# Second block, latent mixer and its memory attention: rotary and memory scores from stacks of high parts and remainders over all 128 rows

## The reference, cut to what matters

```python
def mla_mixer(z, cos, sin, qa_g, kva_g, w_uq, w_ukv, qn_g, kn_g):
    ...
    q = rms_norm_2(q, qn_g)
    k = rms_norm_2(k, kn_g)
    q = jnp.concatenate([q[..., :MLA_NOPE], apply_rope(q[..., MLA_NOPE:], cos, sin)], axis=-1)
    k = jnp.concatenate([k[..., :MLA_NOPE], apply_rope(k[..., MLA_NOPE:], cos, sin)], axis=-1)
    o = causal_block_attention(q, k, v)

def memory_attention(qm, mem_n, w_mem_kv, qn_g, kn_g):
    kv = mem_n @ w_mem_kv
    q = rms_norm_2(qm.reshape(B, S, MEM_HEADS, MEM_HDIM), qn_g)
    k = rms_norm_2(kv[..., :MEM_W].reshape(B, M, MEM_HEADS, MEM_HDIM), kn_g)
    ...
```

## Time and profile before

| | |
|---|---|
| median of three runs | 1678.35 us (1676.62 to 1679.75) |
| profiled execution | 1679.82 us, its span 1678.0 us |
| TensorE | busy 1660.4 us (99%), granted clock 0.998 |
| VectorE, ScalarE, GpSimd | busy 896.8, 781.1, 704.5 us |
| HBM | 150.15 MB read, 91 GB/s over the span |

### The profile page before, as it was taken

How to read it: one execution, slowest core, us unless ns; L and a number is a source line. 1 busy time by engine, 2 the same in 40 slices (tenths; PEclk the granted TensorE clock), 3 DMA queues, 4 the chain that set the end, 5 groups by cost and what they waited for, 6 DMA issues and landing times.

```text
span 1678.0 us, 24465 instructions
## 1 busy us (share of the span) xinstructions
PE 1660.4 (99%) x8381; PEld 1361.3 (81%) x8381; DVE 896.8 (53%) x1718; ACT 781.1 (47%) x1213; POOL 704.5 (42%) x372
## 2 busy tenths in 40 slices
PE   9999999999999999999999999999999999999999
PEld 6788678888987899888888888888767888888887
DVE  6799877558426487646555531152554555555100
ACT  6323566337454545445545432345564455445222
POOL 4344212444634576344444444444202444444445
PEclk9999999999999999999999999999999999999999
DMA  6233211433422210233333333322201323333333
GB/s 223 76 113 107 76 39 62 153 100 104 137 89 88 76 39 26 64 89 100 100 92 96 99 101 101 112 95 88 64 1 51 89 100 100 96 91 100 101 113 113
DMA packets 44381, 153.56 MB, mean 92 GB/s; under 512 B 4976, under 2 KB 5104, under 8 KB 44272
## 3 DMA queue, kind: packets, MB, share of 16 engines
q1 hardware_dynamic: 41184, 145.10, 27.9%
q10 hardware_dynamic: 3120, 7.43, 1.3%
HBM read 150.15 MB, written 2.10 MB: 91 GB/s over the span
## 4 chain that ended last, share of the span: by engine, by line
PE 88%; DVE 4%; issue 4%; POOL 2%; ACT 1%; DMA 0%; POOLq 0%; SPq 0%; ACTq 0%; DVEq 0%
PE DB L1179 9%; PE DB L1178 9%; PE DB L1177 9%; PE DB L744 8%; PE DB L746 8%; PE DB L745 8%; PE DB L1196 5%; PE DB L1198 5%; PE DB L1197 5%; PE SC L873 3%; PE SC L1059 2%; PE DB L893 2%; PE DB L797 2%; POOL WL L644 1%; PE DB L799 1%
## 5 line engine op out<-in xcount | busy, mean ns | idle before, releaser
L644 POOL TENSOR_TENSOR WL<-RAW,WH 128x1024 fp32r<-128x1024 f32 x257 | 618.5, 2407 | 924.8 <-ACT WH L1306 922.1
L1306 ACT ACTIVATE WH<-RAW 128x1024 fp32r<-128x1024 f32 x257 | 272.4, 1060 | 597.5 <-PE DB L746 177.8
L1177 PE MATMUL DB<-XH,WH 128*128 128x512 f32 x640 | 249.0, 389 | 0.0
L1178 PE MATMUL DB<-XL,WH 128*128 128x512 f32 x640 | 249.0, 389 | 0.0
L1179 PE MATMUL DB<-XH,WL 128*128 128x512 f32 x640 | 249.0, 389 | 0.0
L744 PE MATMUL DB<-XH,WH 128*128 128x512 f32 x568 | 228.8, 403 | 3.8 <-POOL WL L644 2.3
L746 PE MATMUL DB<-XH,WL 128*128 128x512 f32 x568 | 221.7, 390 | 0.0
L745 PE MATMUL DB<-XL,WH 128*128 128x512 f32 x568 | 221.4, 390 | 0.0
L1178 PEld LDWEIGHTS DB<-XL,WH 128*128 128x128 f32 x640 | 120.1, 188 | 25.1
L1177 PEld LDWEIGHTS DB<-XH,WH 128*128 128x128 f32 x640 | 120.1, 188 | 24.9
L1179 PEld LDWEIGHTS DB<-XH,WL 128*128 128x128 f32 x640 | 120.1, 188 | 24.9
(11 more groups left out here) (517 smaller groups left out, 2947.9 us busy)
## 6 DMA issues: line engine op xcount, KB each, us to landing
RAW<-in_stream_dram SPq DMA_DIRECT2D x267, 512.0 KB, 3.5
TP<-in_toep_dram ACTq DMA_DIRECT2D x4, 512.0 KB, 3.6
X<-in_xt_dram ACTq DMA_DIRECT2D x1, 2048.0 KB, 13.8
out_dram<-X SPq DMA_DIRECT2D x8, 256.0 KB, 4.3
X<-in_xt_dram ACTq DMA_DIRECT2D x4, 256.0 KB, 6.4
X<-in_xt_dram SPq DMA_DIRECT2D x4, 256.0 KB, 6.1
MRAW<-in_memt_dram ACTq DMA_DIRECT2D x2, 512.0 KB, 4.8
CONST<-in_consts_dram SPq DMA_DIRECT2D x1, 448.0 KB, 8.8
```

What stands on the lines that cost most here:

```text
L644: nc.gpsimd.tensor_tensor(WL[:, s, :], RAW[:, j, :], WH[:, s, :].bitcast(F32), ALU.subtract).then_inc(lo_done, 1)
L1177: mm(o, WH[:, s, c], xh(k), start=(k == 0), stop=False)
L1178: mm(o, WH[:, s, c], xl(k), start=False, stop=False)
L1306: A(WH[:, n % SPLIT, :], RAW[:, n % RING, :], ACT.Copy).then_inc(hi_done, 1)
```

## The change

- The memory queries of layer 1 are stacked: `QMS1` holds for each head its 64 rows rounded, and in the other 64 rows their remainders. The memory keys are held twice, rounded in both halves of the rows (`MKH1`) and as remainders in both halves (`MKL1`). A memory score is now two products of the fast float type over 128 rows, with `MKH1` and with `MKL1`. The two heads no longer wait for one another.
- The rotary queries are stacked in the same way (`QRS`, one tile a head), and the rotary keys, now made over all 128 rows (`KRD` in place of `KR`), are split into `KRH` and `KRL`. A latent score is the float32 product of `QN` and `KN` as before, and two fast products over 128 rows.
- ACT rounds (2 + 4 instructions for the memory, 6 + 6 in `rope_high` for the rotary parts), DVE takes the remainders (4 + 4, and 6 + 6 in `rope_low`). The place of each in its engine's list is seen in the diff. New semaphores join them. The stacks and keys lie where `XH` and `XL` lay, and in free parts of the arena.

```diff
@@ -325,7 +325,6 @@
         QN = at("QN", [P, MLH, TOK], A0 + 0)
         KN = at("KN", [P, MLH, TOK], A0 + 16)
         QR = at("QR", [P, 3, TOK], A0 + 32)
-        KR = at("KR", [P, 3, TOK], A0 + 38)
         MV = at("MV", [P, NT, MLH * P], A0 + 44)
         CQH = at("CQH", [P, 3, TOK], A0 + 44, F32R)
         CQL = at("CQL", [P, 3, TOK], A0 + 50, F32R)
@@ -342,6 +341,13 @@
         POSI = at("POSI", [P, TOK], A0 + 84, I32)
 
         KPR = at("KPR", [P, TOK], A0 + 60)
+        QRS = [at(f"QRS{h}", [P, TOK], A0 + kb, F32R) for h, kb in enumerate((38, 40, 42, 84, 86, 70))]
+        KRD = at("KRD", [P, MLH, TOK], 32)
+        KRH = at("KRH", [P, MLH, TOK], 16, F32R)
+        KRL = at("KRL", [P, MLH, TOK], 32, F32R)
+        QMS1 = at("QMS1", [P, 4, TOK], A0 + 62, F32R)
+        MKH1 = at("MKH1", [P, 4, MEM], 28, F32R)
+        MKL1 = at("MKL1", [P, 4, MEM], 44, F32R)
         YLM = at("YLM", [P, 2, TOK], A0 + 68, F32R)
         HALF = [slice(0, DH), slice(DH, P)]
 
...
@@ -550,7 +564,10 @@
                         r = slice(DH * e, DH * e + DH)
                         h = 2 * p + e
                         c = 8 * p + 2 * i + e
-                        yield dict(rq=RQM[:, c:c + 1], both=RQM[:, c - e:c - e + 2], qk=[(q[r, p, P * i:P * i + P], MKT[l][r, p, :])], w=MEM,
+                        qk = [(q[r, p, P * i:P * i + P], MKT[l][r, p, :])]
+                        if l == 1:
+                            qk = [(QMS1[:, h, P * i:P * i + P], k[:, h, :]) for k in (MKH1, MKL1)]
+                        yield dict(rq=RQM[:, c:c + 1], both=RQM[:, c - e:c - e + 2], qk=qk, w=MEM,
                                    bias=CZ[:, 0:MEM],
                                    v=[MVT[l][:, s, DH * h:DH * h + DH] for s in range(2)],
                                    bank=MOUT[l][p], o=MOUT[l][p][r, P * i:P * i + P], first=(i == 0 and e == 0), last=(i == NT - 1 and e == 1),
@@ -560,12 +577,13 @@
             for j in range(0, MLH, 2):
                 for i in range(NT):
                     for e in range(2):
-                        h, r = j + e, HALF[e]
+                        h = j + e
                         w = P * (i + 1)
                         c = 8 * (h // 2) + 2 * i + h % 2
                         yield dict(rq=HR[:, GROUPS["qn"][0] % 2, c, :],
                                    both=HR[:, GROUPS["qn"][0] % 2, c - e:c - e + 2, 0], qk=[(QN[:, h, P * i:P * i + P], KN[:, h, 0:w]),
-                                       (QR[r, h // 2, P * i:P * i + P], KR[r, h // 2, 0:w])], w=w,
+                                       (QRS[h][:, P * i:P * i + P], KRH[:, h, 0:w]),
+                                       (QRS[h][:, P * i:P * i + P], KRL[:, h, 0:w])], w=w,
                                    bias=CZ[:, TOK - w:TOK],
                                    v=[MV[:, s, P * h:P * h + P] for s in range(i + 1)],
                                    bank=OUT2[e], o=OUT2[e][:, P * i:P * i + P], first=(i == 0), last=(i == NT - 1),
@@ -866,13 +884,17 @@
                         if pair[0]["kind"] == "b" and pair[0]["first"]:
                             pe.wait_ge(kb_low, 1)
                             pe.wait_ge(qs_low, 2 * pair[0]["grp"] + 2)
-                        for a in range(len(pair[0]["qk"])):
-                            for s in pair:
-                                if s["kind"] == "m1" and s is pair[1]:
-                                    pe.wait_ge(qk_done, s["g"])
-                                last = mm(s["score"][:, 0:s["w"]], *s["qk"][a], start=(a == 0), stop=(a == len(s["qk"]) - 1))
-                                if a == len(s["qk"]) - 1:
-                                    last.then_inc(qk_done, 1)
+                        if pair[0]["kind"] == "m1":
+                            pe.wait_ge(mk_low, 4)
+                            pe.wait_ge(qm_low, 4)
+                        if pair[0]["kind"] == "l" and pair[0]["first"]:
+                            pe.wait_ge(kr_low, pair[1]["grp"] + 1)
+                            pe.wait_ge(qr_low, pair[1]["grp"] + 1)
+                        parts = range(len(pair[0]["qk"]))
+                        for a, s in ([(a, s) for s in pair for a in parts] if pair[0]["kind"] == "m1" else itertools.product(parts, pair)):
+                            last = mm(s["score"][:, 0:s["w"]], *s["qk"][a], start=(a == 0), stop=(a == len(s["qk"]) - 1))
+                            if a == len(s["qk"]) - 1:
+                                last.then_inc(qk_done, 1)
                     for _ in range(pieces(k) if beside is not None else 0):
                         next(beside, None)
                     if twos and k >= 4 and k % 2 == 0:
@@ -1762,8 +1784,13 @@
                 head_square(HEADS[f"kn{h}"][1][0], KN[:, h, :])
             evac("qm11", QM1[:, 1, :])
             evacuated("qm11")
+            for e, r in enumerate(HALF):
+                A(QMS1[r, e:4:2, :], QM1[r, :, :], ACT.Copy).then_inc(qm_high, 1)
             for k in range(2):
                 head_square(HEADS[f"qm1{k}"][1][0], QM1[:, k, :])
+            for e, r in enumerate(HALF):
+                for half in (r, HALF[1 - e]):
+                    A(MKH1[half, e:4:2, :], MKT[1][r, :, :], ACT.Copy).then_inc(mk_high, 1)
 
             def key_factors(*heads):
                 for h in heads:
@@ -1777,6 +1804,15 @@
                 b = DB[JOBS[f"uqr{k // 2}"].bank(k % 2)]
                 head_square(HEADS[f"qn{2 * k}"][1][1], b[:, :])
                 A(QR[:, k, :], b[:, :], ACT.Identity, scale=col("qn", 1)).then_inc(act_emptied, 1)
+            def rope_high(k):
+
+                act.wait_ge(roped, 10 + k)
+                for e, r in enumerate(HALF):
+                    A(QRS[2 * k + e][r, :], QR[r, k, :], ACT.Copy).then_inc(qr_high, 1)
+                for h in (2 * k, 2 * k + 1):
+                    act.wait_ge(hs_done, HEADS[f"kn{h}"][0] + 1)
+                    A(KRH[:, h, :], KRD[:, h, :], ACT.Copy).then_inc(kr_high, 1)
+
             kn = HR[:, GROUPS["kn"][0] % 2, 0:24, 0]
             act.wait_ge(kn_sum, 1)
             A(kn, kn, ACT.Sqrt, scale=1.0 / 192).then_inc(kn_std, 1)
@@ -1793,6 +1829,7 @@
                     head_square(HEADS[f"qn{h}"][1][0], QN[:, h, :])
                 if k < 2:
                     key_factors(2 * k + 2, 2 * k + 3)
+                rope_high(k)
             act.wait_ge(kv_std, 1)
             def head_values(k):
                 act.wait_ge(slab_used, JOBS[f"uv{k}"].done)
@@ -2462,20 +2499,42 @@
             V.tensor_tensor(kn.rearrange("p (h t) -> p h t", t=NT), SC[0][:, c:c + 24].rearrange("p (h t) -> p h t", t=NT),
                             KS[:, :, :].broadcast_to([P, MLH, NT]), ALU.add).then_inc(kn_sum, 1)
             query_sums("qm1")
+            for e, r in enumerate(HALF):
+                dve.wait_ge(qm_high, e + 1)
+                for p in range(2):
+                    V.tensor_tensor(QMS1[HALF[1 - e], 2 * p + e, :], QM1[r, p, :], QMS1[r, 2 * p + e, :].bitcast(F32),
+                                    ALU.subtract).then_inc(qm_low, 1)
             dve.wait_ge(kn_std, 1)
             V.reciprocal(kn, kn).then_inc(kn_root, 1)
             rope(9, QR[:, 0, :], COSM[:, :], SINM[:, :], TB[:, :], (rot_done, 6))
 
             def keys(*heads):
                 for h in heads:
-                    r, half = head_root(f"kn{h}"), HALF[h % 2]
+                    r = head_root(f"kn{h}")
                     link(V.scalar_tensor_tensor(KN[:, h, :], KN[:, h, :], GAINQK, r, ALU.mult, ALU.mult))
-                    V.tensor_tensor(KR[half, h // 2, :], KPR[half, :], r[half], ALU.mult).then_inc(hs_done, 1)
+                    V.tensor_tensor(KRD[:, h, :], KPR[:, :], r, ALU.mult).then_inc(hs_done, 1)
+
+            def rope_low(k):
+                for e, r in enumerate(HALF):
+                    dve.wait_ge(qr_high, 2 * k + e + 1)
+                    V.tensor_tensor(QRS[2 * k + e][HALF[1 - e], :], QR[r, k, :], QRS[2 * k + e][r, :].bitcast(F32),
+                                    ALU.subtract).then_inc(qr_low, 1)
+                for h in (2 * k, 2 * k + 1):
+                    dve.wait_ge(kr_high, h + 1)
+                    V.tensor_tensor(KRL[:, h, :], KRD[:, h, :], KRH[:, h, :].bitcast(F32), ALU.subtract).then_inc(kr_low, 1)
 
             rope(10, QR[:, 1, :], COSM[:, :], SINM[:, :], TB[:, :], (rot_done, 7))
             keys(0, 1)
             rope(11, QR[:, 2, :], COSM[:, :], SINM[:, :], TB[:, :], (rot_done, 8))
-            keys(2, 3, 4, 5)
+            keys(2, 3)
+            for e, r in enumerate(HALF):
+                dve.wait_ge(mk_high, 2 * e + 2)
+                for half in HALF:
+                    V.tensor_tensor(MKL1[half, e:4:2, :], MKT[1][r, :, :], MKH1[r, e:4:2, :].bitcast(F32),
+                                    ALU.subtract).then_inc(mk_low, 1)
+            keys(4, 5)
+            for k in range(3):
+                rope_low(k)
             query_roots("qm1")
             dve.wait_ge(hs_ss, max(HEADS[f"qn{h}"][1][0] for h in range(MLH)) + 1)
```

8 lines of the change are left out of this document (added).

## The result

| | before | changed |
|---|---|---|
| median | 1678.38 us (1676.54 to 1681.26, 20 runs) | 1681.24 us (1680.66 to 1682.80, 20 runs) |
| profiled execution, its span | 1679.82, 1678.0 us | 1682.37, 1680.3 us |
| granted clock, mean of the span | 0.998 | 0.995 |
| ratio | | 1.0016, 95% interval 1.0010 to 1.0022 |

The changed kernel is 0.16% slower, 2.9 us. That lies within the 0.2% (its interval reaches to 0.22) that the prediction called no change, but on the other side of zero than the forecast of -1.15 us, and 0.04 us above the range. Rival A, held up twice with a clock fall behind it, gave 1681.9.

A forecast was written before the change was run, and what follows sets the result against it. TensorE, busy 99% of the span, was taken as the bound; start +1.6, memory pairs -1.0 and -1.45, rotary -0.3 sum to -1.15 us, giving 1677.2 us from the median, range 1673.8 to 1681.2 us.

The forecast's parts named there:

- Rival A: Remainders on DVE held up twice by POOL, then PE's clock falls: +2.5 to +4 us, about 1681.9; chance 0.15.
- the start: Stretch up to the first values product: DVE's 20 new remainders delay the first read of scores, costing 1.6 us.
- Memory scores, 0.56 us a pair: PE's memory scores: four fast matmuls take 0.56 us instead of 1.38, 0.82 less in each of eight pairs.
- What PE can use of it: Memory pairs: second of each group gains 0.48 us, first of group one 1.0, first of groups two and three 0.
- Rotary scores, 0.3 us in all: PE's twelve rotary pairs: 0.3 us gained in all, between a loss of 0.5 and a gain of 2.4.
- The start, four remainders of the memory queries: cost 0: DVE behind the sums at 1165 us, idle around the next rotation: cost 0; bad end 1 us late on PE.
- The start, four key remainders: cost 0 if nothing holds them up: DVE's memory-key remainders, 2.4 us, fit into its 2.64 us of idle ahead of 1190.42: cost 0 if not held up.
- the first half of A: POOL holds the fourth memory-key remainder, last keys 2.1 us later; alone +1.0 us in sum, 1679.3, chance 0.18.
- The start, twelve remainders, 0.61 us apart plus one hold: DVE's rotary remainders between last key and roots: 7.3 us, then held by POOL to about 1202.7 to 1203.0.
- First read of scores at 1204.7: DVE's first read of attention scores comes at 1204.7, 2.6 us later than 1202.11.
- From the first read to the first values product, 6.3 us: ACT's chain of exponentials, moves and copy behind the first read; PE's first values product waits until 1211.0.
- The clock: PE's clock at the start: no fall in the forecast; behind over 4 us of idle, 1.5 to 3 us more.

The follow-up runs named there:

- e1: Changed kernel plus 20 fast matmuls with discarded results on PE just ahead of the second memory pair's scores; 1680.83 us, ratio 1.0009 to the kernel before.
- e3: Changed kernel with the rotary part taken back, only the memory scores in the new form; 1676.11 us, ratio 0.9987 to the kernel before.
- e6: Changed kernel with eight of twelve rotary remainders moved between attention pairs, memory-key remainders left in place; 1676.77 us, ratio 0.9989 to the kernel before.
- e7: Changed kernel plus 32 fast matmuls with discarded results on PE just ahead of the second memory pair's scores; 1679.63 us, ratio 1.0007 to the kernel before.
- e2: Changed kernel with only the four memory-key remainders moved to directly behind keys of heads 0 and 1; 1679.44 us, ratio 1.0003 to the kernel before.
- e10: e9 with ScalarE's four moves of the second half of the memory values put ahead of the first exponential; 1676.76 us.
- e12: Kernel before, with only ScalarE's four moves of the second half of the memory values put ahead of the first exponential; 1682.63 us, ratio 1.0025.
- e5: Changed kernel with eight rotary remainders moved between attention pairs and memory-key remainders one rotation earlier; 1676.25 us, ratio 0.9981 to the kernel before.
- e9: e5 with the eight moved rotary remainders placed one at a time in VectorE's gaps; 1674.70 us, ratio 0.9980 to the kernel before.
- e4: Changed kernel with the memory part taken back, only the rotary scores in the new form; 1681.21 us, ratio 1.0011 to the kernel before.
- e8: e3 with the four memory-key remainders moved to directly behind keys of heads 0 and 1; 1675.94 us, ratio 0.9982 to the kernel before.
- e11: Rotary scores alone in the new form, eight of their twelve remainders moved between attention pairs; 1677.73 us, ratio 0.9997 to the kernel before.

## Why the prediction was wrong

The step that failed is the start, put at +1.6 us: it cost 4.2 us, because the four key remainders were held, which the sum had at nothing, and the fall of the clock behind it, also at nothing there, cost another 2.7. The gains were larger than forecast and made up for part of it. Point by point, by its own steps:

- **Memory scores, 0.56 us a pair.** Right: 0.47 measured where PE goes on at once.
- **What PE can use of it.** Right in both waits: 1.12 us behind the first m of groups two and three (gain 0), 0.43 behind the second m's (0.34 forecast, three times). The second m pair is 0.23 us shorter in place of 0.48 (1244.94 to 1246.09, against 1.38), and the transposes ahead of each of the two m pairs give 0.18 that the forecast did not have.
- **Rotary scores, 0.3 us in all.** Mis-sized. The 512-key pair is 0.24 us shorter; by width, 128 to 384 keys, the pairs take 0.93, 1.34 and 2.09 us in place of 0.96, 1.59 and 2.24. That is 0.67 a group, 2.0 in all, near the good bound of 2.4, and for the reason named there: the rotary part itself costs 0.26 us more (1.32 for 1.06) and its float32 neighbour 0.50 less (1.31 for 1.81). The step compared the 64-row product with the stack on its own, while the price of the 64-row form stood in the row of the product ahead of it. The Trainium skill (TensorEngine Tiling (Array Packing), Overview and Key Properties) says that a change of tiling mode drains the engine; leaving the 64-row products out took 0.5 us off the neighbour here, which fits, though no record names a drain.
- **The start, four remainders of the memory queries: cost 0.** Right. They were held too, 4.77 us, but with VectorE idle behind them nothing came of it.
- **The start, four key remainders: cost 0 if nothing holds them up.** Failed. This is the step with which the loss begins. They were held, 4.89 us in place of 2.4, and the next keys came 2.3 us late. The prediction had that as the first half of A and took the other side of a tie of half a microsecond. In all five profiled executions that keep them at that place (the changed kernel, e1, e3, e6, e7) they took 4.89 to 4.94 us.
- **The start, twelve remainders, 0.61 us apart plus one hold.** Mis-sized. They took 10.4 us in place of 9.6: the hold came, but they stand 0.69 apart (four of them from 1195.61 to 1198.37). The spacing of 0.61 had been read from the two `YL` of the earlier trace rows.
- **First read of scores at 1204.7.** It was 1207.49: 2.3 late by the keys, 0.8 by the twelve, 0.3 regained behind them.
- **From the first read to the first values product, 6.3 us.** The chain was right: 1213.65 - 1207.43 = 6.22 where the clock stays up (e7). In the changed kernel it was 7.92, by the clock.
- **The clock.** Failed: put at nothing in the forecast. The prediction expected a fall only behind the idle of over 4 us that both holds make. Of the profiled executions a fall comes in or behind an idle of 5.2 us of idle in the changed kernel, 4.5 in e2, 3.3 in e10, 2.8 in e12, 2.5 in e1, 1.9 in e5, e6 and e9, and 1.7 in e4; none comes with 1.9 in e3 and e8, 1.6 in e7 and 1.4 in e11. The length alone does not tell, but the forecast's own 2.3 us of idle should have carried a chance of a fall and a price.
- **Sum.** Start +4.2 without the clock (1213.65 in e7 against 1209.48) where the forecast had 1.6; clock +2.7 where it had nothing; and from the first values product to `wo10` the groups give back 4.5 (1266.44 - 1213.65 = 52.8 us in e7, 57.3 before), where it had 2.75 for all gains. That is +2.3 at `wo10`, as in the changed kernel's trace; the medians say +2.9.
- **Chances.** Rival A in full had 0.15, and gave 1681.9 against 1681.24 measured and 1682.37 profiled. Its mechanism is the one that came, its number is in part luck: start and clock cost 6.9 us in place of its 5.2 to 6.7, and the gains were 4.5 in place of 2.75. It tied the fall to the held keys; in e2 and e4, where the last keys were not late, the clock fell too.
- The other side of the range was nearer than it looked: with the same work placed otherwise, e9 stands at 1674.7.

## What to carry to other kernels

Work put on an engine that is off the path is free only until the next point where the bounding engine waits for it. Twelve small subtractions on VectorE, ahead of an attention's first scores, and four held ones before them, turned a gain of 4 us into a loss of 3; with eight of them between the attention's pairs and the four a rotation earlier the gain came back. So place such work by due time, not by kind. And price a new idle of TensorE at its length plus a clock fall that may follow (2.7 us here); and before moving work into an idle of ScalarE, look when its input is there and which table load will come behind it.

## What the runs showed of the hardware that was not expected

- **The times of one kernel come in steps, and the steps go with the clock.** The kernel before, measured 33 times beside e1 to e4, gave for each mean granted clock a narrow group: 1.000 1676.47 to 1676.66 us (5 runs), 0.999 1678.01 to 1678.52 (12), 0.998 1679.46 to 1680.09 (8), 0.997 1681.17 to 1681.70 (8). So some 1.6 us a step, with nothing between. The changed kernel's 20 runs lie at 0.994 to 0.997 and never above; with the 32 matmuls (e7) it is 0.998 to 0.999 again. What decides which group an execution falls in was not tried. The places where the clock differs between executions of the same work are two, near 1174 and 1190 us, each behind sums of squares, 24 and 16 products of two columns and of one (from 1169.89 and 1187.94 in the kernel before): in e1 and e3 it stayed at 1.00 there, in the profiled executions of before and after it did not.
- **GpSimd's subtraction holds up even a 2-column instruction.** In e5 a scale of two columns, which takes 0.16 us elsewhere, took 1.86:

```profile
1210.08 2.35 POOL L662 TENSOR_TENSOR WL<-RAW,WH 128x1024 fp32r<-128x1024 f32 x1 [7.92 <-ACT WH L1328]
...
1210.58 1.86 DVE L2005 SCALAR_TENSOR_TENSOR ST<-ST,HR 128x2 f32<-128x2 f32 x1
```

  It ended at 1212.44, GpSimd's at 1212.43. In the kernel before the same instruction took 2.33 us (begun at 1210.46, GpSimd's at 1210.42). A read of scores from PSUM that stood inside GpSimd's subtraction in e9 (begun at 1208.38, GpSimd's at 1208.29) took its usual 0.42 us. The Trainium skill (SBUF — State Buffer, SBUF: two separate sides) says that a VectorE instruction with two SBUF inputs and a GpSimd one that reads SBUF exclude one another for the whole length; the rows agree, and show that the price does not hang on the size of the held instruction.
- **The hold goes both ways.** In e5 the four key remainders, one rotation earlier, took 2.83 us and GpSimd's subtraction of 1181.42 2.79 instead of 2.35; in e8 it was 2.84 and 2.66. At the same place in e2 and e9 they took 4.95 and 4.92. So there, and not where the change has them, which of the two comes first differs from one kernel to the next.
